# Expert weights of a mixture-of-experts stage loaded with adjacent rows per partition, and the two stationary operands read with a step to match

## What is computed

```python
def hier_moe(h, w_rg, b_rg, w_re, b_re, w_gate, w_up, w_down):
    ...
    gate = g_onehot[:, :, None] * (p_top * gate_in)[:, None, :]
    y = jnp.zeros((n * length, d), f32)
    for gi in range(N_GROUPS):
        hid = jax.nn.silu(jnp.einsum('td,edf->tef', x, w_gate[gi])) * jnp.einsum('td,edf->tef', x, w_up[gi])
        y = y + jnp.einsum('tef,efd->td', hid * gate[:, gi, :, None], w_down[gi])
    return y.astype(h.dtype).reshape(n, length, d)
```

## Time and profile before

| what | value |
|---|---|
| median of 3 runs | 1719.01 us (1716.60 to 1725.06) |
| profiled execution, span from first to last instruction | 1715.5 us |
| the median less that span | 3.5 us |
| TensorE (PE) busy | 1535.0 us, 89% |
| TensorE weight load (PEld) busy | 1225.9 us, 71% |
| VectorE (DVE) busy | 873.0 us, 51% |
| ScalarE (ACT) busy | 705.7 us, 41% |
| SP's DMA queue (q1) | 235860 packets, 287.43 MB, 50.2% of 16 engines |

### The profile page before, as it was taken

One profiled execution on the slowest core, in us unless ns is written; L12 is line 12 of the kernel. 1 busy time (PEld: TensorE's weight loads), 2 busy tenths in 40 slices (PEclk: granted clock), 3 DMA queues, 4 the chain that ended last, 5 costly groups with the idle time before them and its releaser, 6 DMA issues.

```text
span 1715.5 us, 23319 instructions
## 1 busy us (share of the span) xinstructions
PE 1535.0 (89%) x8812; PEld 1225.9 (71%) x8812; DVE 873.0 (51%) x1443; ACT 705.7 (41%) x1039; POOL 89.5 (5%) x122
## 2 busy tenths in 40 slices
PE   5799999988969999999859999999996999999984
PEld 2598776633646888888739967778764688888873
DVE  1472434022244888888643242333214588888862
ACT  0462111000024877777534321211112587777742
POOL 0000010000000000001000010000000000001000
PEclk9899999888969999999979997887796999999997
DMA  9532135444303999999824463443120499999930
GB/s 283 156 122 66 50 96 175 152 154 147 123 25 100 332 331 330 331 332 321 274 60 139 147 229 123 137 142 132 57 81 18 135 332 329 332 333 321 317 107 32
DMA packets 247506, 317.57 MB, mean 185 GB/s; under 512 B 9088, under 2 KB 224160, under 8 KB 247414
## 3 DMA queue, kind: packets, MB, share of 16 engines
q1 hardware_dynamic: 235860, 287.43, 50.2%
q0 software_dynamic: 7120, 26.32, 4.8%
q10 hardware_dynamic: 4434, 2.59, 0.6%
HBM read 309.82 MB, written 6.49 MB: 184 GB/s over the span
## 4 chain that ended last, share of the span: by engine, by line
PE 64%; issue 21%; DVE 7%; ACT 5%; POOL 2%; ACTq 1%; DMA 0%; DVEq 0%; POOLq 0%
PE bank L1023 10%; PE bank L984 8%; PE bank L952 7%; PE bank L954 7%; PE bank L953 7%; PE bank L947 3%; PE bank L1275 3%; PE bank L1055 2%; PE bank L1390 2%; DVE wl L2209 2%; PE bank L1255 2%; PE bank L1277 2%; PE bank L1325 2%; PE bank L993 1%; POOL arena L822 1%
## 5 line engine op out<-in xcount | busy, mean ns | idle before, releaser
L2209 DVE TENSOR_TENSOR wl<-ring,wh 128x1024 fp32r<-128x1024 f32 x384 | 486.8, 1275 | 85.9 <-ACT wh L1458 79.3
L1458 ACT ACTIVATE wh<-ring 128x1024 fp32r<-128x1024 f32 x422 | 444.8, 1060 | 157.7 <-PE bank L954 154.4
L952 PE MATMUL bank<-wh,hgh 128*128 128x256 f32 x1024 | 298.1, 291 | 24.5 <-DVE wl L2209 24.3
L953 PE MATMUL bank<-wl,hgh 128*128 128x256 f32 x1024 | 291.2, 284 | 0.0
L954 PE MATMUL bank<-wh,hgl 128*128 128x256 f32 x1024 | 291.1, 284 | 0.0
L952 PEld LDWEIGHTS bank<-wh,hgh 128*128 128x128 f32 x1024 | 197.5, 193 | 31.9 <-DVE wl L2209 28.8
L953 PEld LDWEIGHTS bank<-wl,hgh 128*128 128x128 f32 x1024 | 197.9, 193 | 0.6
L954 PEld LDWEIGHTS bank<-wh,hgl 128*128 128x128 f32 x1024 | 197.5, 193 | 0.0
L1023 PE MATMUL bank<-ring,condT 128*9 128x256 f32 x768 | 182.5, 393 | 11.1 <-ACT condT L1725 11.1
L1458 ACT ACTIVATE arena<-bank 128x512 f32<-128x512 f32 (+4 forms) x150 | 64.4, 460 | 244.2 <-PE bank L947 77.1
L1023 PEld LDWEIGHTS bank<-ring,condT 128*9 128x9 f32 x768 | 67.9, 93 | 106.5 <-issue 13.0
(11 more groups left out here) (285 smaller groups left out, 2051.3 us busy)
## 6 DMA issues: line engine op xcount, KB each, us to landing
ring<-in_w_exp_gate_dram SPq DMA_DIRECT2D x64, 1024.0 KB, 5.4
ring<-in_w_exp_up_dram SPq DMA_DIRECT2D x64, 1024.0 KB, 5.3
ring<-in_w_exp_down_dram SPq DMA_DIRECT2D x64, 1024.0 KB, 5.0
ring<-in_w_ada_dram SPq DMA_DIRECT2D x48, 1024.0 KB, 5.3
ring<-in_w_in_even_dram SPq DMA_DIRECT2D x14, 1024.0 KB, 5.2
ring<-in_w_qkv_odd_dram SPq DMA_DIRECT2D x12, 1024.0 KB, 5.6
arena<-in_cache_c_k_dram POOLq DMA_DIRECT2D x8, 1024.0 KB, 5.6
arena<-in_cache_c_v_dram POOLq DMA_DIRECT2D x8, 1024.0 KB, 5.2
```

The source lines that it names most:

```text
L952: pe.matmul(out, a[0], b[0], start=start, stop=False)
L953: pe.matmul(out, a[0], b[1], start=False, stop=False)
L1458: return act.activation(dst, src, ACT.Copy)
L2209: dve.tensor_tensor(wl[:, h % NH, :], unit[:, U // 2 * (h % 2):U // 2 * (h % 2) + U // 2], wh[:, h % NH, :].bitcast(F32), ALU.subtract).th ...
```

## The change

The three views of the expert weights give each partition adjacent rows, eight of a gate or up matrix and two of a down matrix, which is one run of 2048 floats (8 KB) in memory. The DMAs then have whole ring slots as destination. Partition p holds rows 8 p to 8 p + 7 of gate and up, and 2 p and 2 p + 1 of down; so chunk c of the gather takes every eighth column of `htok` from c on, and block f of the transposes every second column of `hid` from f on. Counts of instructions, waits, slots and the order stay as they were. (The second path changes in the same way.)

```diff
-        gate_v = I["w_exp_gate"].rearrange("l g e (c p) f -> (l g e) p c f", p=P)
-        up_v = I["w_exp_up"].rearrange("l g e (c p) f -> (l g e) p c f", p=P)
-        down_v = I["w_exp_down"].rearrange("l g e (f p) d -> (l g e) p f d", p=P)
-        expert_views = [(gate_v, 256), (up_v, 256), (down_v, D)]
+        gate_v = I["w_exp_gate"].rearrange("l g e (p c) f -> (l g e) p (c f)", p=P)
+        up_v = I["w_exp_up"].rearrange("l g e (p c) f -> (l g e) p (c f)", p=P)
+        down_v = I["w_exp_down"].rearrange("l g e (p f) d -> (l g e) p (f d)", p=P)
+        expert_views = [gate_v, up_v, down_v]
...
-                sp.dma_start(slot(n, width), src).then_inc(unit_loaded[n % R], 16)
+                dst = slot(n, width) if width < U else ring[:, n % R, :]
+                sp.dma_start(dst, src).then_inc(unit_loaded[n % R], 16)
...
-                        src = view[bass.ds(4 * q + (NG * NE * l + u), 1)].rearrange("a p c f -> p (a c) f")
-                        sp.dma_start(slot(base + p, width), src).then_inc(unit_loaded[(base + p) % R], 16)
+                        src = expert_views[w][bass.ds(4 * q + (NG * NE * l + u), 1)].rearrange("a p n -> p (a n)")
+                        sp.dma_start(ring[:, (base + p) % R, :], src).then_inc(unit_loaded[(base + p) % R], 16)
...
-                            ins = pe.matmul(bk[:, :], htok[0:m, t, P * (a - 4):P * (a - 4) + P],
+                            ins = pe.matmul(bk[:, :], htok[0:m, t, a - 4:D:C],
                                             perm[0:m, t, :, :].rearrange("p g s -> p (g s)"),
                                             start=(t == 0), stop=(t == 2))
...
                                 ins = pe.transpose(bank[2][:, 256 * (u % 2) + P * f:256 * (u % 2) + P * f + P],
-                                                   hid[:, u % 2, P * f:P * f + P], I_(P))
+                                                   hid[:, u % 2, f:DE:2], I_(P))
```

More of the change, by code:

```diff
@@ L753, in load_experts @@
                 for p, (u, w) in enumerate(STREAM):
-                    view, width = expert_views[w]
-                    load(base + p, view[NG * NE * l + u], width)
+                    load(base + p, expert_views[w][NG * NE * l + u], U)
                 with sp.Fori(1, NG * NE // 4) as q:
                     for p, (u, w) in enumerate(STREAM):
-                        view, width = expert_views[w]
                         sp.wait_ge(moe["lo"], HALVES * q + (PASS_HALVES * l + 2 * (p - R) + 2))
-                        src = view[bass.ds(4 * q + (NG * NE * l + u), 1)].rearrange("a p c f -> p (a c) f")
-                        sp.dma_start(slot(base + p, width), src).then_inc(unit_loaded[(base + p) % R], 16)
+                        src = expert_views[w][bass.ds(4 * q + (NG * NE * l + u), 1)].rearrange("a p n -> p (a n)")
+                        sp.dma_start(ring[:, (base + p) % R, :], src).then_inc(unit_loaded[(base + p) % R], 16)
                 after(sp, "dve", f"flag{l}")
@@ L770, in load_experts @@
                             for p, (u, w) in enumerate(STREAM):
-                                view, width = expert_views[w]
                                 if p >= 3:
                                     sp.wait_ge(S["lo"], 2 * (p - 3) + 2)
-                                sp.dma_start(slot(p % 3, width), view[NG * NE * l + u]).then_inc(S[f"wl{p % 3}"], 16)
+                                sp.dma_start(ring[:, p % 3, :], expert_views[w][NG * NE * l + u]).then_inc(S[f"wl{p % 3}"], 16)
                         with sp.Fori(1 - i, NG * NE // 4) as q:
                             for p, (u, w) in enumerate(STREAM):
-                                view, width = expert_views[w]
                                 sp.wait_ge(S["lo"], HALVES * q + (PASS_HALVES * i + 2 * (p - 3) + 2))
-                                src = view[bass.ds(4 * q + (NG * NE * l + u), 1)].rearrange("a p c f -> p (a c) f")
-                                sp.dma_start(slot(p % 3, width), src).then_inc(S[f"wl{p % 3}"], 16)
+                                src = expert_views[w][bass.ds(4 * q + (NG * NE * l + u), 1)].rearrange("a p n -> p (a n)")
+                                sp.dma_start(ring[:, p % 3, :], src).then_inc(S[f"wl{p % 3}"], 16)
                     sp.wait_ge(S["lo"], 2 * PASS_HALVES)
```

## The result

The changed kernel takes 1726.41 us (median of 5 runs, 1724.31 to 1730.13) against 1719.01 us (median of 5). The ratio is 1.0041 with a 95% interval of [1.0022, 1.0059]: slower by about 7 us, clear of zero. The ratio lies within the 0.5% that was called no change; the upper end of its interval, 0.59%, does not. In a second comparison the same kernel had 1727.45 us and 1.0044 [1.0027, 1.0061].

The account below looks back on a forecast made before the run. TensorE was taken to bound the expert stages, not the transfers. Terms 0 + 3.2 + 0 = +3.2 us on a profiled span of 1715.5 us gave 1718.7, forecast as a median of 1722 us (+0.2%), range 1712 to 1733.

Parts of the forecast that it names:

- no change: On the total time: a difference within about 0.5%, some 8.6 us; forecast with its no-op twin had chance 0.82.
- The transfers: Expert weight loads: longer HBM runs land earlier, gate from 5.4 to about 5.0 us or less, gaining 0 us.
- a group: Expert stages: two loop iterations, eight experts, taken as 76.5 us and forecast at 76.5 to 76.8 us.
- the cover: Weight ring in the expert loops: a load has about 14.7 us before its data are needed, and needs 7.0 at worst.
- The rival that the queue would cut the long runs as finely as before: Expert weight loads: gate still lands at 5.4 us, time 1719 to 1722; chance 0.05, inside "same".
- the faster rival: Expert stages: transfers are the bound after all, longer runs give back at most 39 us, 1680 us; chance 0.05.
- The gather: Gather's fp32 products: weight loads in steps of 8 floats cost more where not hidden, +3.2 us, bound 10.6 us.
- the 32 exposed loads: Gather: two unhidden weight loads in each of 8 chunks in 2 layers, each 0.10 us longer.
- The window forecast: Profile window of the gather: near 27.5 us instead of 25.9, with weight loads above 0.19 us.
- The transposes: 128 transposes of the hidden columns, loaded in steps of 2: taken as 0, with 13.4 us kept for the range.
- The slower rival: Transposes of the hidden columns: step 2 doubles a load, +13.4 us, with the gather 1735.6 us; chance 0.13.
- The sum: Whole kernel: 0 for transfers, +3.2 us for gather, 0 for transposes, so +3.2 us in all.

Follow-up runs that it names:

- the layout alone: All three expert weights with adjacent rows, but gather and transposes reading contiguous columns as in the kernel before: 1722.56 us, 1.0014 [1.0002, 1.0026] against that kernel.

## Why the prediction was right

**The transfers** were put at 0, and that was right in each step: landings fell to 4.8 us (5.0 or less forecast), the DMA share from 0.97 to 0.88, and SP's wait grew. With the layout alone the loops took as long as before. The 76.5 us that the prediction gives a group are the length of the window it had laid. By POOL's additions a group, two iterations, takes 76.8 us in the kernel before (620.24 to 697.03) and with the layout alone (619.17 to 695.96), and 77.0 in the changed kernel (623.13 to 700.17), by the transposes. The estimate of the cover (14.7 us of which 7.0 are needed) was borne out: with 12.8 us of it gone the transfers set the pace. The rival that the queue would cut the long runs as finely as before falls with the packets and with gate's landing. The Trainium skill (DMA: Bandwidth & Descriptors, section Why small descriptors are slow), cited for the faster rival, agrees in its direction: 9% less DMA time at the same rate, more than the 7.5% that were estimated by it for rows of 1 KB. That the rate was not the limit is what kept this from the time.

**The gather** was put at +3.2 us by a doubling of the time in which a load's columns stream, taken from a VectorE reduction in the same step. Measured: a load longer by 0.124 us, two exposed loads in a chunk, 0.25 us a chunk. The price was low by a fifth. The count was high by four: of the 32 exposed loads the four in the first chunks run at the lower clock, where the step costs next to nothing. That makes 3.6 us, so part of the agreement is two small errors that work against each other. The window forecast (27.5 us) came out as 27.9 and 29.6; the second has a lower mean clock, and the forecast had compared it with the lucky one of the two gathers of before.

**The transposes** are the term that was mis-sized: 0 was taken, with a doubling (13.4 us) kept for the range. Measured: a load of 0.204 us instead of 0.139, of which 0.04 us per pair show, 0.13 us an iteration, 2.1 us in all. The slower rival needed a load of over 0.21 us, and the load stopped just short. The step that failed was the argument that a step of 2 lies nearer to none than to 8; nothing in the trace of before priced it. For the gather's loads it holds (0.31 us for two instead of 0.29), for the transposes' it does not. A second step failed the other way: a slower load was to count in full, which would have added 128 x 0.065 = 8.3 us, and about a quarter of it shows.

**The sum** of the two loads is then 3.6 + 2.1 = 5.7 us where 3.2 were forecast, and about 7 were measured; the 1.4 us between are less than the granted clock moves from run to run, and their cause stays open. The time is inside the range and the direction came out as the sum had it. But the forecast of 1722 us was 4.4 us low, more than the cost that it named, and what it called no change is a slowdown that repeated runs can tell from none.

The cacheline rule of the Trainium skill (SBUF — State Buffer, section on Door 1) said that steps of 8 floats pay and steps of 2 don't. The gather's loads at the higher clock agree: 0.29 us for two at step 1, 0.31 at 2, 0.42 at 3, flat from 4 on. The transposes' loads don't: 0.139 to 0.204 us at step 2.

## What to carry to other kernels

Before a transfer is reshaped, look at who waits for it: a DMA share of 0.97 said nothing here, while a landing time near that of a load that often runs alone and an issuing queue that waits for free slots said that a faster transfer would only wait longer. A layout that saves the queue work and makes an operand of a matmul stepped is paid by the engine on the path, so count the weight loads that no matmul covers. And with kernels whose stages move by 2 to 4 us between executions, read a small effect in its own stage, at a like granted clock, and not in the total.

## What was not expected of the hardware

- A contiguous weight load of a transpose takes 0.139 us and one of an fp32 product 0.189; in steps of 2 they take 0.204 and 0.20. The shorter one loses its lead.
- At the lower granted clock a step of 8 hardly lengthens the gather's loads: two back to back take 0.55 us instead of 0.50, where at the higher clock they take 0.55 instead of 0.29.
- ScalarE's copy of 512 columns out of PSUM takes 597 ns when it writes a run and 1077 ns when it writes every 128th float.
- The same stage of the same kernel took 443.3 us in one execution and 447.3 in another, at a mean granted clock of 0.86 and 0.85.
